# The expert results' store to HBM moves from SyncE's plain transfer to an indirect transfer of GpSimd

## The reference

```python
def _moe(x, router_w, router_bias, w_gate, w_up, w_down, sh_gate, sh_up, sh_down):
    t = x.reshape(bsz * l, d)                                # 640 tokens in both streams, d = 1024
    scores = jax.nn.sigmoid((t @ router_w).astype(jnp.float32))
    _, idx = lax.top_k(scores + router_bias, TOP_K)          # 8 of 64 experts for each token
    sel = jnp.take_along_axis(scores, idx, axis=-1)
    wts = sel / jnp.sum(sel, axis=-1, keepdims=True) * ROUTED_SCALE
    gates = jnp.einsum('tk,tke->te', wts, jax.nn.one_hot(idx, N_EXPERTS))
    hid = jax.nn.silu(jnp.einsum('td,edf->tef', t, w_gate)) * jnp.einsum('td,edf->tef', t, w_up)
    routed = jnp.einsum('tef,efd->td', hid * gates[..., None], w_down)     # f = 128
    shared = (jax.nn.silu(t @ sh_gate) * (t @ sh_up)) @ sh_down
    return (routed + shared).reshape(bsz, l, d)
```

## Time and profile before

| | |
|---|---|
| Time, median of 3 runs | 1611.73 us (1608.58 to 1612.01) |
| The profiled execution | 1608.47 us, its span 1606.6 us |
| PE busy | 1445.9 us (90%), 8256 instructions |
| DVE busy | 706.1 us (44%) |
| ACT busy | 403.0 us (25%) |
| POOL busy | 317.4 us (20%), 450 instructions |
| Moved by DMA | 279.76 MB; HBM written 64.52 MB |
| Chain that ended last | PE 35%; POOL 3%; issue 3%; DMA 2% |

### The profile page before, as it was taken

How to read it: one execution, slowest core, us unless ns; L and a number is a source line. 1 busy time by engine, 2 the same in 40 slices (tenths; PEclk the granted TensorE clock), 3 DMA queues, 4 the chain that set the end, 5 groups by cost and what they waited for, 6 DMA issues and landing times. The chain is left out here.

```text
span 1606.6 us, 21724 instructions
## 1 busy us (share of the span) xinstructions
PE 1445.9 (90%) x8256; PEld 1057.5 (66%) x8256; DVE 706.1 (44%) x1268; ACT 403.0 (25%) x773; POOL 317.4 (20%) x450
## 2 busy tenths in 40 slices
PE   5999999996899999788779798989999999999955
PEld 1565895854788898555445553768888888888712
DVE  2615572038466655477756511524222222222246
ACT  2211100132654555322113100332122121121101
POOL 0200000010322120234435211011121111211164
PEclk9999989998899999999979899979999999999987
DMA  9624532100390000100001140039999999999787
GB/s 360 190 89 131 175 114 78 54 1 0 127 420 18 1 1 1 30 11 1 27 33 55 51 166 0 27 107 406 373 391 376 387 383 396 390 391 352 253 314 288
DMA packets 101057, 279.76 MB, mean 174 GB/s; under 512 B 22609, under 2 KB 39251, under 8 KB 99580
## 3 DMA queue, kind: packets, MB, share of 16 engines
q1 hardware_dynamic: 85148, 235.55, 40.0%
q0 software_dynamic: 15840, 43.28, 7.1%
HBM read 230.97 MB, written 64.52 MB: 184 GB/s over the span
## 5 line engine op out<-in xcount | busy, mean ns | idle before, releaser
L2505 PEld LDWEIGHTS PS<-arena 128*128 128x128 f32 x2240 | 258.9, 192 | 41.5 <-ACT arena L2989 23.2
L2505 PE MATMUL PS<-arena 128*128 128x128 f32 x2240 | 262.7, 276 | 4.2 <-DMA arena<-in_exp_w_down 2.9
L689 PE MATMUL PS<-arena 128*128 128x512 f32 x384 | 175.6, 612 | 1.5 <-DVE arena L1149 1.5
L2808 DVE TENSOR_SCALAR arena<-PS,arena 128x1024 f32<-128x1024 f32 x70 | 89.9, 1284 | 141.6 <-PE PS L2513 141.6
L2513 PE MATMUL PS<-arena 128*128 128x512 f32 x280 | 137.8, 614 | 0.8 <-DVE arena L2801 0.8
L689 PEld LDWEIGHTS PS<-arena 128*128 128x128 f32 x384 | 74.0, 197 | 87.9 <-issue 86.8
L2801 DVE TENSOR_TENSOR arena<-arena,PS 128x128 f32<-128x128 f32 x70 | 20.2, 288 | 181.3 <-ACT arena L2995 181.3
L2995 ACT ACTIVATE arena<-PS 128x128 f32<-128x128 f32 x70 | 19.4, 277 | 311.4 <-PE PS L2505 311.4
L701 PE MATMUL PS<-arena 128*128 128x256 f32 (+1 forms) x400 | 88.5, 388 | 0.0
L1049 PEld LDWEIGHTS PS<-arena 64*128 64x128 f32 x640 | 43.6, 195 | 62.9 <-issue 30.5
L701 PEld LDWEIGHTS PS<-arena 128*128 128x128 f32 x400 | 77.7, 215 | 9.8
(11 more groups left out here) (456 smaller groups left out, 2253.4 us busy)
## 6 DMA issues: line engine op xcount, KB each, us to landing
arena<-in_exp_w_gate SPq DMA_DIRECT2D x70, 512.0 KB, 6.0
arena<-in_exp_w_up SPq DMA_DIRECT2D x70, 512.0 KB, 13.0
arena<-in_exp_w_down SPq DMA_DIRECT2D x70, 512.0 KB, 16.4
y_rows<-arena SPq DMA_DIRECT2D x70, 512.0 KB, 17.1
y_rows<-cst SPq DMA_DIRECT2D x1, 21504.0 KB, 58.2
arena<-in_w_in SPq DMA_DIRECT2D x16, 1024.0 KB, 6.5
arena<-in_w_mod SPq DMA_DIRECT2D x32, 512.0 KB, 3.5
arena<-in_w_mod SPq DMA_DIRECT2D x4, 2048.0 KB, 15.2
```

What stands on the lines that cost most here:

```text
L689: pe.matmul(PS[:, b0, :], w[:, k, i * P:(i + 1) * P], hT[:, k, 0:SMP], start=(k == 0), stop=(k == KT - 1))
L2505: mm = pe.matmul(PS[:, bank, 0:P], w[:, k, :], xT[j % 2][:, k, :], start=k == 0, stop=k == KT - 1)
L2808: dve.tensor_scalar(yb[j].rearrange("p (h n) -> p h n", h=2), PS[:, 4 + 2 * (j % 2):6 + 2 * (j % 2), :], gate_col[j % 2], None, ALU.mult). ...
```

## The change

`store_block` leaves SP and is written anew on POOL. It copies the block's column of a new table `store_row` into a small tile (`tensor_copy`), and stores `yb` with an indirect transfer, whose bounds check leaves out rows whose index is beyond `y_rows`. `store_row` holds 128 b + slot for a full slot, and a number beyond the bound for an empty one. DVE makes it with one operation ahead of L2751 and three behind L2795. On POOL each fetch is followed by a store: fetch of block b, then store of block b-4 (in the spill: of block b-2). The fill at L554 covers the rows of all 106 blocks instead of the last 42.

```diff
--- before.py
+++ after.py
@@ -550,8 +550,8 @@
                 for m, n in enumerate(("gdn_norm_g", "hgrn_norm_g", "mlstm_norm_g")):
                     sp.dma_start(norm_row[:, m, :], T[n].to_broadcast([P, HD])).then_inc(n_in, 16)
 
-                y_spill = T["y_rows"].rearrange("(b p) d -> p b d", p=P)[:, NE:, :]
-                sp.dma_start(y_spill, spread(at["strict"][:, 0:D], 1, COLS - NE)).then_inc(tail_out, 16)
+                y_all = T["y_rows"].rearrange("(b p) d -> p b d", p=P)
+                sp.dma_start(y_all, spread(at["strict"][:, 0:D], 1, COLS)).then_inc(tail_out, 16)
 
                 sp.wait_ge(m_otaken, len(UNITS))
                 sp.wait_ge(g_otaken, len(UNITS))
@@ -2098,6 +2098,8 @@
         token_row = kept(COLS).bitcast(U32)
         block_expert = kept(P + 1)[0:1].bitcast(U32)
         token_col = [kept(1).bitcast(U32) for _ in range(U)]
+        store_row = kept(COLS).bitcast(U32)
+        store_col = [kept(1).bitcast(U32) for _ in range(U)]
         dest_u = kept(PAIRS).bitcast(U32)
         gate_col = [kept(1) for _ in range(2)]
         D1 = kept(NT * NE).rearrange("p (t n) -> p t n", t=NT)
@@ -2109,6 +2111,7 @@
             taken[0] += words
             assert taken[0] <= r1_at + 8192
             return part(taken[0] - words, words)
+        row_no, no_row = (part(r1_at + 8192 - COLS * i, COLS) for i in (1, 2))
         off = scratch((NT + 1) * NE).rearrange("p (t n) -> p t n", t=NT + 1)
         cum = [scratch(2 * NE) for _ in range(2)]
         biased = scratch(NT * NE).rearrange("p (t n) -> p t n", t=NT)
@@ -2134,6 +2137,7 @@
         g_in = [sem(f"g_in{i}") for i in range(GB)]
         s_w, s_gu, s_up, s_act, s_hid, s_ps, s_acc = (sem("s_" + n) for n in "w gu up act hid ps acc".split())
         h2_out, x_col, m_dest = sem("h2_out"), sem("x_col"), sem("m_dest")
+        y_col = sem("y_col")
         e_w, e_x = [sem(f"e_w{j}") for j in range(U)], [sem(f"e_x{j}") for j in range(U)]
         e_tr, e_xT, e_gc, e_gu, e_silu, e_hid, e_ps, e_y = (sem("e_" + n) for n in "tr xT gc gu silu hid ps y".split())
         e_out = [sem(f"e_out{j}") for j in range(U)]
@@ -2171,7 +2175,6 @@
                 sp.dma_start(fin_row, T["final_g"].rearrange("(a n) -> a n", a=1).to_broadcast([P, D])).then_inc(o_fg, 16)
                 wg = T["exp_w_gate"].rearrange("a e (p k) f -> p (a e) k f", k=KT)
                 wu = T["exp_w_up"].rearrange("a e (p k) f -> p (a e) k f", k=KT)
-                y_rows = T["y_rows"].rearrange("(b p) d -> p b d", p=P)
                 wd = T["exp_w_down"].rearrange("a e f d -> f (a e) d")
 
                 sp.dma_start(eg[1], T["sh_w_gate"].rearrange("a (p k) f -> p (a k) f", k=KT)).then_inc(s_w, 16)
@@ -2184,10 +2187,6 @@
                     sp.dma_start(eg[j], wg[:, bass.ds(e, 1)].rearrange("p a k f -> p (a k) f")).then_inc(e_w[j], 16)
                     sp.dma_start(eu[j], wu[:, bass.ds(e, 1)].rearrange("p a k f -> p (a k) f")).then_inc(e_w[j], 16)
                     sp.dma_start(ed[j], wd[:, bass.ds(e, 1)].rearrange("p a d -> p (a d)")).then_inc(e_w[j], 16)
-
-                def store_block(b, j):
-                    sp.wait_ge(e_y, b + 1)
-                    sp.dma_start(y_rows[:, bass.ds(b, 1)].rearrange("p b d -> p (b d)"), yb[j]).then_inc(e_out[j], 16)
 
                 load_block(0, 0)
                 for t in range(NT):
@@ -2205,7 +2204,6 @@
                     for j in range(U):
                         sp.wait_ge(e_ps, U * i + (j + 1 - U))
                         load_block(U * i + j, j)
-                        store_block(U * i + (j - U), j)
 
                 def spill_load(s, j, free):
                     e = sp.value_load(block_expert[0:1, bass.ds(s, 1)], min_val=0, max_val=NE - 1)
@@ -2215,15 +2213,9 @@
                 groups = group_count(sp)
                 for j in range(2):
                     spill_load(j, j, NE - U + 1 + j)
-                    store_block(NE - U + j, j)
-                for j in range(2, U):
-                    store_block(NE - U + j, j)
                 with sp.Fori(1, groups) as i:
                     for j in range(2):
                         spill_load(2 * i + j, j, 2 * i + (NE - 1 + j))
-                        store_block(2 * i + (NE - 2 + j), j)
-                for j in range(2):
-                    store_block(2 * groups + (NE - 2 + j), j)
                 for t in range(NT):
                     sp.wait_ge(f_y, t + 1)
                     dst = T["y_sample"].rearrange("a (t p) d -> p (a t) d", p=P)[:, t] if t < 4 else T["y_prompt"][0]
@@ -2748,6 +2740,7 @@
                     s *= 2
                 incl, excl = a[:, NE:], a[:, NE - 1:2 * NE - 1]
 
+                dve_order.done(dve.tensor_scalar(row_no, iota[:, 0:COLS], float(P), slot_no, ALU.mult, ALU.add))
                 dve_order.done(dve.tensor_scalar(cmpb, incl, slot_no, None, ALU.is_le))
                 dve.tensor_reduce(ecol, cmpb, AX.X, ALU.add).then_inc(m_ecol, 1)
 
@@ -2793,6 +2786,9 @@
 
                 dve.wait_ge(m_tab, NT)
                 dve.tensor_scalar(token_row, PS[:, 6, 0:COLS], float(TOK), None, ALU.add).then_inc(m_tok, 1)
+                dve_order.done(dve.tensor_scalar(no_row, PS[:, 6, 0:COLS], -0.5, float(COLS * P), ALU.is_ge, ALU.mult))
+                dve_order.done(dve.tensor_tensor(row_no, row_no, no_row, ALU.add))
+                dve.tensor_copy(store_row, row_no).then_inc(y_col, 2 * U)
 
                 def hidden(b, j, e):
                     dve.wait_ge(e_xT, b + 1)
@@ -3091,17 +3087,36 @@
                     pool.indirect_dma_start(xg[j], None, T["h2_rows"], bass.IndirectOffsetOnAxis(token_col[j], 0),
                                             bounds_check=TOK - 1, oob_is_err=False).then_inc(e_x[j], 16)
 
+                def store_block(b, j):
+
+                    pool.wait_ge(e_y, b + 1)
+                    pool.wait_ge(y_col, 2 * U)
+                    done = b + (2 * U + 1)
+                    pool.compute_val(done)
+                    pool.tensor_copy(store_col[j], store_row[:, bass.ds(b, 1)]).then_inc(y_col, 1)
+                    pool.wait_ge(y_col, 2 * U)
+                    pool.wait_ge(y_col, done)
+                    pool.indirect_dma_start(T["y_rows"], bass.IndirectOffsetOnAxis(store_col[j], 0), yb[j], None,
+                                            bounds_check=COLS * P - 1, oob_is_err=False).then_inc(e_out[j], 16)
+
                 for j in range(U):
                     fetch_x(j, j)
                 with pool.Fori(1, NE // U) as i:
                     for j in range(U):
                         fetch_x(U * i + j, j, U * i + (j - U + 1))
+                        store_block(U * i + (j - U), j)
                 for j in range(2):
                     fetch_x(NE + j, j, NE - U + j + 1)
+                    store_block(NE - U + j, j)
+                for j in range(2, U):
+                    store_block(NE - U + j, j)
                 groups = group_count(pool)
                 with pool.Fori(1, groups) as i:
                     for j in range(2):
                         fetch_x(2 * i + (NE + j), j, 2 * i + (NE - 1 + j))
+                        store_block(2 * i + (NE - 2 + j), j)
+                for j in range(2):
+                    store_block(2 * groups + (NE - 2 + j), j)
 
                 stored = 16 * groups + 16 * (NE // U)
                 pool.compute_val(stored)
```

## The result

The changed kernel takes 1645.55 us in the median of 4 runs (1640.99 to 1652.38); the kernel before takes 1611.35 us beside it. The ratio is 1.0219, 95% interval 1.0174 to 1.0264: slower by some 34 us. The prediction was 1613.6 us, in a range of 1608.5 to 1618.5. The profiled execution took 1640.99 us, its span is 1639.1 us.

A forecast was written before the change was run, and what follows sets the result against it. PE was taken to bound the steady blocks, with DMA full but early. Bytes, POOL, buffers, spill, fill and DVE at 0 plus 1.9 us for the last store gave 1611.73 + 1.9 = 1613.6 us, range 1608.5 to 1618.5.

The forecast's parts named there:

- the weights: SP's weight loads land earlier without stores: 0 in steady blocks, already early; in the spill 1.4 us, at most 4.04.
- Bytes: Expert stage: stores shrink by 15.7 MB, worth 0 because PE is full in steady blocks; at most -1 us.
- The first rival: Faster: the spill's weight stall falls, -4.0 us, steady blocks -1.0, last store +1.5: 1608.2 us; chance 0.15.
- HBM written up by 33.6 - 15.7 MB: Sign expected in the profile after: HBM writes grow with the larger fill, less the 15.7 MB of rows left out.
- POOL's issue and the order on POOL: Steady blocks: store and fetch take 4.06 of 6.32 us on POOL; the delayed fetch has 10 us of cover: 0.
- `yb` buffers: Expert blocks: the indirect store lands in 9 us, before the buffer's reuse after 22.7 us: cost 0.
- The spill: Last five blocks: earlier weights offset by fetches losing their cover; value 0, ends -4.0 and +5 us.
- The second rival: Slower: POOL's order bounds the spill once fetches land at 8.6 us, +5.3, plus 1.9 at the end: 1618.9 us; chance 0.27.
- The last store: Behind the last block: copy and index delay the transfer, landing takes 3.4 us, first gather later: +1.9 us.
- The fill, DVE: Fill lands after 138 us, hidden behind the mixers: 0; four small DVE operations: 0, at most 0.3 us each.
- if PE shows idle time in steady blocks: Stated sign of being wrong: the forecast had PE full in the steady expert blocks at 6.32 us a block.

The follow-up runs named there:

- E4: The changed kernel, but POOL stores all 128 rows of each block with a plain transfer, no index or column copy: 1641.66 us, ratio 1.0175.
- E1: The changed kernel, but with every row in bounds, so that POOL's indirect store writes all 128 rows: 1647.29 us, ratio 1.0212.
- E6: The kernel before, but ACT issues the whole-tile stores, each behind the Silu of the next block: 1621.75 us, ratio 1.0072.
- E7: The changed kernel with a plain POOL store of all 128 rows and slots spread over the partitions: 1612.12 us, ratio 1.0009.
- E11: The kernel before, but ACT issues whole-tile stores behind the next block's Silu, with slots spread over the partitions: 1605.41 us, ratio 0.9981.
- E5: The kernel before with only the large fill, covering the rows of all 106 blocks: 1610.49 us, ratio 1.0004.
- E12: The kernel before, but ACT issues the whole-tile stores ahead of the Silu, slots in order: 1622.84 us, ratio 1.0069.
- E2: The changed kernel with slot s of a block on partition 4 (s mod 32) + s div 32: 1610.04 us, ratio 0.9978.
- E3: The kernel before, SP storing whole tiles, with slot s on partition 4 (s mod 32) + s div 32: 1611.24 us, ratio 0.9986.

## Why the prediction was wrong

The step that failed is *the weights*: "In steady blocks they are early already: 0." I read from the earlier trace rows that PE is full and concluded that the loads have cover, without counting it; and I took the store's leaving SP's queue to make them land earlier. They landed later, 20.0 us instead of 16.5, and PE waited 28.7 us for them. The loads of block b are issued when the down products of block b-4 are done, beside the gate and up products of block b-3, and are used three blocks behind those. In the block of the earlier trace rows:

```profile
1307.36 3.73 PE L2505 MATMUL PS<-arena 128*128 128x128 f32 x32
...
1308.60 1.34 SPq L2186 DMA_DIRECT2D arena<-in_exp_w_down  x1
```

1307.36 + 3 x 6.32 - 1308.60 = 17.7 us from the third load's issue to its use. Its landing was 16.5 us, 1.2 us of cover. It was creeping up as well. Landings of the third load before, in windows 1100 to 1110, 1150 to 1250 and 1350 to 1450:

```profile
arena<-in_exp_w_down SPq DMA_DIRECT2D x2, 512.0 KB, 13.3
...
arena<-in_exp_w_down SPq DMA_DIRECT2D x16, 512.0 KB, 16.2
...
arena<-in_exp_w_down SPq DMA_DIRECT2D x16, 512.0 KB, 17.6
```

At 17.6 us nothing of the cover is left. The sum that I didn't make goes by one engine: a sixteenth of the fill's 417 GB/s is 26.1 GB/s. If each engine has 8 of the 128 partitions, an engine whose 8 fetched rows are all full has for each block 32 rows of 4,096 B and 8 of 4,352 B, 166 KB: 6.36 us, for a block of 6.32. In the changed kernel it has 24 rows of 4,096 B (weights), 8 of 4,352 B and 8 of 4,096 B (store), the same 166 KB: no relief. Spread evenly, 5,120 pairs are 5 rows an engine and block, 24 x 4,096 + 5 x 8,448 B = 141 KB, 5.4 us. By this estimate the full engines stand at their limit in both kernels, and anything that makes a packet dearer goes straight into the time. With the queue something did: E4's 28 us over 64 blocks are 0.45 us a block for 8 of such an engine's 40 rows.

Point by point:

- *Bytes.* 0 forecast, and E1 against the changed kernel measures 0 within their intervals. But the reason given, that PE is full, was wrong: it is that the rows left out weren't on the engines that mattered. 15.7 MB is a mean over engines. The first rival, in which the steady blocks gain 1.0 us, had the same fault. Of the signs, "HBM written up by 33.6 - 15.7 MB" can't be read as I meant it: the page gives 98.08 MB after 64.52, up by 33.6, and 98.08 in E1 too, so that count holds the rows left out as well. What the packets moved does show them: 297.60 MB after 279.76, up by 17.8, and 313.31 in E1.
- *The queue.* Not priced at all. I priced POOL's issue and the order on POOL, both rightly (cover was there, no wait for fetches), and took a row to cost the same on either queue. E4, E6, E7 and E11 show it: +28 us on POOL's, +11 to +12 on ACT's, none that can be told where the engines have room.
- *`yb` buffers.* Landing 7.8 us, 9 taken; no stall. Right.
- *The spill.* 0 forecast, -1.3 us measured in one execution, near the 1.4 us that I had for loads alone; the fetches were in time. The second rival, with the largest chance of a loss, was the wrong place: no line of waits names the fetch.
- *The last store.* +1.9 forecast, +0.5 measured. I took 3.4 us for the landing of a nearly empty store; it landed in 2.1. The 2.0 us that the Trainium skill gives as fixed ("DMA: Bandwidth & Descriptors", section "Anatomy of one DMA"), against which I argued from a gather of 512 KB, was the better figure, and the trace agrees with it here.
- *The fill, DVE.* 0, and 0 measured for the fill (E5). DVE's four operations were not run by themselves; the last of them ends at 1067.56, 11 us ahead of the first gate and up products at 1078.59.
- What I named as proof of being wrong, "if PE shows idle time in steady blocks", is what the profile shows.

What is open: by what a store on POOL's queue, and less so on ACT's, takes more of the full engines' time. E12 excludes the moment of issue for ACT's. The indirect form may add something, 1.0212 in E1 after 1.0175 in E4, but the intervals touch. A rival that no run tests is the order of service: on SP's queue a store stood behind loads, in a queue of its own its packets can go before loads issued earlier. Order alone would move work, not add any, and the trace speaks for added work, though it doesn't show it. In the changed kernel new loads are issued every 6.9 us (441.1 us for 64 blocks) while the last step of a block's loads takes 20.0 us, so the engine that ends last has loads before it all the time; and yet by the estimate above it moves 166 KB in 6.9 us, 24.1 GB/s, where it moved them in 6.32 before.

The changed kernel with spread slots, E2, takes 0.9978 (0.9962 to 0.9994) of the kernel before, at the edge of what can be told. E3 gives 0.9986 (0.9974 to 0.9998) with SP's plain stores, so that no gain of the change itself is shown.

## What to carry to other kernels

Where loads land late beside full DMA, count their cover (from issue to use, less the landing) before calling them hidden, and make the sum for the fullest DMA engine, not for the mean of 16. Tiles that were filled from partition 0 up crowded their rows on some of the engines here; leaving rows out relieved the others. Spreading rows over the partitions cost seven small operations here and took away a loss of 34 us.

## What the runs showed of the hardware

- Moving the same whole-tile stores from SP's queue to POOL's cost 28 us (E4), and to ACT's 11 to 12 us (E6), where slots stood in order. It cost nothing that can be told where they were spread (1.0009 in E7 and 0.9981 in E11, beside 0.9986 in E3 with SP's stores).
- Where the full rows of a tile lie among its partitions changed the time with the same bytes and queues: 1.0219 in order, 1.0218 reversed, 0.9978 spread. The last part of a block's loads landed after 17.3 us in order (E12) and 10.2 spread (E11).
- A row left out by the bounds check still is a packet: 25,920 packets on POOL's queue after the change for 180 transfers, 144 for each, with 64.27 MB, and as many with 79.98 MB in E1.
- A DMA share of 0.97 to 1.02 stood beside 349 to 388 GB/s in these windows. The share says that packets are under way, not that no more can be moved.
